# V rows gathered as 32 tokens of four experts, and multiplied in four column groups of 32

## The reference: what is computed

```
for every token t:
    i[0:128], gate[0:128] = top experts of 8 heads x 16, softmax within a head
    w[e] = gate[e] * gelu(dot(u[i[e]], xn[t]))          # 128 weights
    out[t] = sum over e of w[e] * v[i[e]]               # 128 rows of v
```

## Time and profile before

| | |
|---|---|
| median of the timed runs | 2024.65 us |
| fastest, slowest | 2023.76, 2026.74 us |
| span of the profiled execution, first to last instruction | 2043.0 us |
| PE, DVE, ACT, POOL busy | 95%, 58%, 22%, 43% |
| DMA over the span | 300 GB/s |
| share of the chain that ended last: PE, DMA, DVE, POOL | 65%, 13%, 9%, 7% |

### The profile page before, as it was taken

How to read it: one execution, slowest core, us unless ns; L and a number is a source line. 1 busy time by engine, 2 the same in 40 slices (tenths; PEclk the granted TensorE clock), 3 DMA queues, 4 the chain that set the end, 5 groups by cost and what they waited for, 6 DMA issues and landing times.

```text
span 2043.0 us, 23964 instructions
## 1 busy us (share of the span) xinstructions
PE 1942.4 (95%) x9007; PEld 1255.0 (61%) x9007; DVE 1190.6 (58%) x2972; ACT 445.9 (22%) x1045; POOL 870.7 (43%) x785
## 2 busy tenths in 40 slices
PE   8999999999889999999998888999999989999998
PEld 7688886956775887885676765444445543333332
DVE  1022101003896888788899989887867775444321
ACT  2233211111202454121211354000013321101112
POOL 0000000000684423445658355844557776666543
PEclk9999999999999999999999568999999999999999
DMA  7543454434999877999899677999999999999997
GB/s 237 147 121 109 148 155 144 145 103 136 373 388 349 280 255 239 369 386 388 331 359 371 221 261 243 410 409 409 409 376 348 344 334 410 409 409 409 409 389 278
DMA packets 252439, 613.48 MB, mean 300 GB/s; under 512 B 18676, under 2 KB 121124, under 8 KB 252324
## 3 DMA queue, kind: packets, MB, share of 16 engines
q0 software_dynamic: 110592, 402.70, 52.5%
q1 hardware_dynamic: 141120, 208.17, 29.7%
q10 hardware_dynamic: 612, 1.07, 0.2%
HBM read 609.77 MB, written 2.10 MB: 300 GB/s over the span
## 4 chain that ended last, share of the span: by engine, by line
PE 65%; DMA 13%; DVE 9%; POOL 7%; issue 3%; another core or an unknown queue 1%; ACT 1%; SPq 0%; POOLq 0%; DVEq 0%; ACTq 0%
PE ps L617 26%; PE ps L896 11%; PE ps L846 8%; DMA u_rows<-in_peer_u_dram,idx 7%; PE ps L632 7%; POOL u_rows L576 5%; DVE u_rows L1391 4%; PE ps L886 3%; PE ps L659 3%; POOL v_rows L590 2%; DMA wring<-in_w_in_dram 2%; DMA v_rows<-in_peer_v_dram,idx_turned 2%; PE ps L646 1%; PE ps L685 1%
## 5 line engine op out<-in xcount | busy, mean ns | idle before, releaser
L576 POOL DMA_INDIRECT u_rows<-in_peer_u_dram,idx x512 | 584.5, 1142 | 977.1 <-DVE idx L1378 508.2
L1391 DVE CUSTOM_DVE_ANT_0 u_rows<-u_rows,xn 128x1024 f32<-128x1024 f32 x512 | 621.3, 1217 | 177.8 <-DMA u_rows<-in_peer_u_dram,idx 165.2
L617 PE MATMUL ps<-xT,wring 128*128 128x256 f32 x2432 | 553.1, 386 | 22.3 <-DMA wring<-in_w_in_dram 10.1
L617 PEld LDWEIGHTS ps<-xT,wring 128*128 128x128 f32 x2432 | 464.0, 193 | 90.8 <-DMA wring<-in_w_in_dram 11.0
L896 PE MATMUL ps<-d_rows,gates 128*128 128x512 f32 x1024 | 456.3, 600 | 0.8 <-issue 0.8
L896 PEld LDWEIGHTS ps<-d_rows,gates 128*128 128x128 f32 x1024 | 190.7, 191 | 266.6 <-issue 266.6
L846 PE MATMUL ps<-v_rows,diag 64*64 64x512 f32 x1928 | 256.9, 633 | 18.9 <-DMA v_rows<-in_peer_v_dram,idx_turned 16.4
L590 POOL DMA_INDIRECT v_rows<-in_peer_v_dram,idx x121 | 135.4, 1119 | 131.3 <-PE ps L846 98.6
L886 PEld LDWEIGHTS ps<-hot_b,hot_a 128*128 128x128 f32 x1024 | 147.2, 230 | 55.4 <-issue 36.0
L886 PE MATMUL ps<-hot_b,hot_a 128*128 128x64 f32 x1024 | 155.0, 318 | 19.3 <-DVE hot_b L1458 11.0
L1091 ACT ACTIVATE diag<-ident,wgt 128x64 f32<-128x64 f32 x256 | 75.8, 336 | 435.6 <-PE ps L846 351.5
(11 more groups left out here) (201 smaller groups left out, 1747.0 us busy)
## 6 DMA issues: line engine op xcount, KB each, us to landing
wring<-in_w_in_dram SPq DMA_DIRECT2D x128, 512.0 KB
d_rows<-in_peer_v_dram SPq DMA_DIRECT2D x128, 512.0 KB
wring<-in_peer_w_query_dram SPq DMA_DIRECT2D x32, 512.0 KB
wring<-in_w_branch_conv_dram SPq DMA_DIRECT2D x16, 512.0 KB
wring<-in_w_branch_attn_dram SPq DMA_DIRECT2D x16, 512.0 KB
wring<-in_w_out_dram SPq DMA_DIRECT2D x16, 512.0 KB
wring<-in_xattn_wq_dram SPq DMA_DIRECT2D x16, 512.0 KB
wring<-in_xattn_wo_dram SPq DMA_DIRECT2D x16, 512.0 KB
```

The source lines that it names most:

```text
L576: pool.indirect_dma_start(out=u_rows[:, n % URING, :], out_offset=None, in_=peer_u[0], in_offset=bass.IndirectOffsetOnAxis(ap=experts_of(g ...
L617: mm = pe.matmul(bank(job)[:, 0:HN], w[:, k % 4, P * b:P * (b + 1)], act[:, k, :], start=(k == 0), stop=(k == KT - 1))
L1391: dve.tensor_tensor_reduce(out=u, in0=u, in1=(xn2 if h else xn1)[:, i, :], scale=1.0, scalar=0.0, op0=ALU.mult, op1=ALU.add, accum_out=dot ...
```

## The change

Four V rows are now multiplied at a time (`expert_quad`). V row m of a group no longer holds one expert for 128 tokens. Partition 32q + t of row b of set s (m = 4s + b in the group) holds expert 4q + s of token 32b + t: 32 tokens with four experts each. Its weights stand below each other as four 32x32 diagonals, one tile of 128 rows and 32 columns (`ident32`, scaled by ACT). The matmul with the row sums four experts for 32 tokens and writes PSUM partitions 32b to 32b + 31; the four rows of a quad write the four column groups. A token tile now takes two banks, and the two tiles take different banks.

For this the expert numbers (`idx_quad`) are rearranged by 16 small copies of DVE a group instead of two, the weights by 16 small activations of ACT a group (`spread_weights`), and DVE's three multiplies at the end of `gelu` become one. DVE's step 4 of the next group's `gelu` waits for those activations. `diag` has 12 places of half the width. The V ring has 6 places, 8 from slot 108 of this half, 10 from slot 236, and the U places at the end as before. A place comes free when its quad is done. Diagonals are not made before the slot in which their group's weights are spread (`WEIGHTS_AT`). The slots of chunks, blocks and V rows stay; a quad stands in the slot of its fourth row.

```diff
@@ -167,7 +167,8 @@
     HG = GROUPS // 2
-    URING, VRING, DRING, GRING, IRING = 8, 8, 8, 4, 8
+    URING, VRING, DRING, GRING, IRING = 8, 10, 12, 4, 8
+    BLOCK = P // 4
     CHUNKS, BLOCKS = 64, 128
@@ -184,22 +185,25 @@
     FIN_SLOT = {2: HSTEPS + 225}
-    V_OF, DIAG_OF, PAIR_OF = {}, {}, {}
+    V_OF, DIAG_OF, QUAD_OF = {}, {}, {}
+    WEIGHTS_AT = [HSTEPS + TOPK * (g + 1) + 8 for g in range(HG)]
     for m, slot in enumerate(V_SLOT):
         V_OF.setdefault(slot + V_AHEAD, []).append(m)
-        DIAG_OF.setdefault(slot + (DIAG_BEHIND if slot >= STEPS - 16 else -DIAG_AHEAD), []).append(m)
-        if m % 2:
-            PAIR_OF.setdefault(slot, []).append(m - 1)
-
-
-    V_LATE = next(m for m in range(HSTEPS) if V_SLOT[m] >= CH_SLOT[32])
+        DIAG_OF.setdefault(max(slot + (DIAG_BEHIND if slot >= STEPS - 16 else -DIAG_AHEAD), WEIGHTS_AT[m // TOPK]),
+                           []).append(m)
+        if m % 4 == 3:
+            QUAD_OF.setdefault(slot, []).append(m - 3)
+
+
+    V_GROWS = {next(m for m in range(HSTEPS) if V_SLOT[m] + V_AHEAD > TOPK * (HG + PH * (n + 1) - 1)): n
+               for n in range(HT)}
     V_LAST = next(m for m in range(HSTEPS) if V_SLOT[m] + V_AHEAD >= STEPS + 6)
...
     for m in range(HSTEPS):
-        if m == V_LATE:
-            ring = [("v", n, None) for n in (6, 7)] + ring
+        if m in V_GROWS:
+            ring = [("v", 6 + 2 * V_GROWS[m] + n, None) for n in range(2)] + ring
         if m == V_LAST:
@@ -275,8 +279,8 @@
         probsT = at("probsT", [P, 2, XH, HN], 122)
-        diag = at("diag", [P, DRING, P // 2], 122)
-        ident64 = at("ident64", [P, P // 2], 125)
+        diag = at("diag", [P, DRING, BLOCK], 122)
+        ident32 = at("ident32", [P, BLOCK], 123.5)
         hot_b = at("hot_b", [P, 2, 8, 64], 126)
@@ -325,7 +329,7 @@
         idx = tiny("idx", [P, IRING, TOPK], U32)
-        idx_turned = at("idx_turned", [P, HG, TOPK // 2], 125.25, U32)
+        idx_quad = at("idx_quad", [P, HG, TOPK], 125, U32)
         idx2 = at("idx2", [P, HG, TOPK], 124, U32)
@@ -382,7 +386,8 @@
         idx_rdy = sem("idx_rdy")
-        turned = sem("turned")
+        quad_idx = sem("quad_idx")
+        quad_wgt = sem("quad_wgt")
         gate_rdy = sem("gate_rdy")
@@ -486,7 +491,7 @@
         def wait_used(eng, m):
-            eng.wait_ge(v_used, m // 2 + 1)
+            eng.wait_ge(v_used, m // 4 + 1)
@@ -565,8 +570,12 @@
                     wait_job(pool, JOB[("xo", 1, 1)] + 1)
-                    pool.tensor_tensor(ident64[:, :], ident[:, 0:P // 2], ident[:, P // 2:P],
+                    pool.tensor_tensor(ident32[:, :], ident[:, 0:BLOCK], ident[:, BLOCK:2 * BLOCK],
                                        ALU.add).then_inc(iotas, 1)
+                    for q in (2, 3):
+                        pool.wait_ge(iotas, q + 1)
+                        pool.tensor_tensor(ident32[:, :], ident32[:, :], ident[:, BLOCK * q:BLOCK * (q + 1)],
+                                           ALU.add).then_inc(iotas, 1)
                 if n < STEPS:
@@ -585,11 +594,10 @@
                     if e == 0:
-                        pool.wait_ge(turned, 2 * (g + 1))
-                    own = idx_turned[:, g, e // 2:e // 2 + 1] if e % 2 else idx2[:, g, e:e + 1]
+                        pool.wait_ge(quad_idx, 16 * (g + 1))
                     pool.indirect_dma_start(
                         out=v_row(m), out_offset=None, in_=peer_v[0],
-                        in_offset=bass.IndirectOffsetOnAxis(ap=own, axis=0)
+                        in_offset=bass.IndirectOffsetOnAxis(ap=idx_quad[:, g, e:e + 1], axis=0)
                     ).then_inc((v_ready if kind == "v" else u_ready)[place], 16)
@@ -830,22 +838,18 @@
-            def expert_pair(m):
+            def expert_quad(m):
                 if m == 0:
                     pe.wait_ge(wt_done, 2 * SBH)
-                if m == HSTEPS // 2:
-                    pe.wait_ge(hadd, 2)
-                pe.wait_ge(diag_rdy, m + 2)
-                for k in (m, m + 1):
-                    wait_row(pe, k)
-                first, last = m % (HSTEPS // 2) == 0, m % (HSTEPS // 2) == HSTEPS // 2 - 2
+                tile, n = m // (HSTEPS // 2), m % (HSTEPS // 2)
+                pe.wait_ge(diag_rdy, m + 4)
+                for b in range(4):
+                    wait_row(pe, m + b)
                 for c in range(2):
-                    for k, turn in ((m, 0), (m + 1, 64)):
-                        for r in (0, 64):
-                            o = (r + turn) % P
-                            mm = pe.matmul(ps[o:o + 64, 2 * (r // 64) + c, :], diag[r:r + 64, k % DRING, :],
-                                           v_row(k)[r:r + 64, BANK * c:BANK * (c + 1)],
-                                           start=first, stop=last)
+                    for b in range(4):
+                        mm = pe.matmul(ps[BLOCK * b:BLOCK * (b + 1), 2 * tile + c, :], diag[:, (m + b) % DRING, :],
+                                       v_row(m + b)[:, BANK * c:BANK * (c + 1)],
+                                       start=(n == 0), stop=(n == HSTEPS // 2 - 4))
                 mm.then_inc(v_used, 1)
@@ -905,8 +909,8 @@
                     table_transposes()
-                for m in PAIR_OF.get(tau, []):
-                    expert_pair(m)
+                for m in QUAD_OF.get(tau, []):
+                    expert_quad(m)
                 for ch in range(CHUNKS):
@@ -1080,15 +1084,23 @@
+            def spread_weights(g):
+                act.wait_ge(wgt_rdy, HG + g + 1)
+                for b in range(4):
+                    for q in range(4):
+                        to = wgt[BLOCK * q:BLOCK * (q + 1), g, :].rearrange("p (s b) -> p s b", b=4)[:, :, b]
+                        qw = act.activation(to, gl[BLOCK * b:BLOCK * (b + 1), 3, 4 * q:4 * (q + 1)], ACT.Copy)
+                qw.then_inc(quad_wgt, 1)
+
             def diagonal(m):
...
                 if e == 0:
-                    act.wait_ge(wgt_rdy, HG + g + 1)
+                    act.wait_ge(quad_wgt, g + 1)
                 if m == 0:
-                    act.wait_ge(iotas, 3)
+                    act.wait_ge(iotas, 5)
                 if m >= DRING:
-                    act.wait_ge(v_used, (m - DRING) // 2 + 1)
-                act.activation(diag[:, m % DRING, :], ident64[:, :], ACT.Copy,
+                    act.wait_ge(v_used, (m - DRING) // 4 + 1)
+                act.activation(diag[:, m % DRING, :], ident32[:, :], ACT.Copy,
                                scale=wgt[:, g, e:e + 1]).then_inc(diag_rdy, 1)
@@ -1128,7 +1140,7 @@
                 else:
-                    act.wait_ge(hadd, 2 * (i + 1))
+                    act.wait_ge(hadd, i + 1)
                 inverse_rms(("fin", h, i), hbuf[:, t, :], xn2[:, 0, :])
@@ -1146,6 +1158,8 @@
                     take_tables()
+                if tau in WEIGHTS_AT:
+                    spread_weights(WEIGHTS_AT.index(tau))
                 for m in DIAG_OF.get(tau, []):
@@ -1379,9 +1393,12 @@
                     dve.wait_ge(idx_rdy, g + 1)
-                    odd = idx2[:, g - HG, :].rearrange("p (e two) -> p e two", two=2)[:, :, 1]
-                    for r in (0, 64):
-                        dve.tensor_copy(idx_turned[64 - r:P - r, g - HG, :], odd[r:r + 64, :]).then_inc(turned, 1)
+                    for b in range(4):
+                        for q in range(4):
+                            to = idx_quad[BLOCK * q:BLOCK * (q + 1), g - HG, :].rearrange("p (s b) -> p s b", b=4)
+                            dve.tensor_copy(to[:, :, b], idx2[BLOCK * b:BLOCK * (b + 1), g - HG,
+                                                              4 * q:4 * (q + 1)]).then_inc(quad_idx, 1)
+                        yield
@@ -1414,6 +1431,8 @@
                     dve.wait_ge(gate_rdy, g + 1)
+                    if g > HG:
+                        dve.wait_ge(quad_wgt, g - HG)
                     dve.tensor_tensor(s3, a, gate_e[:, r:r + wide, :], ALU.mult)
@@ -1430,13 +1449,8 @@
                     else:
-                        for odd, p0, turn in ((0, slice(0, P), 0), (1, slice(0, 64), 64), (1, slice(64, P), -64)):
-                            to, a3, a2 = (t[:, k, :].rearrange("p (e two) -> p e two", two=2)[:, :, odd]
-                                          for t, k in ((wgt, g - HG), (s3, 0), (s2, 0)))
-                            ins = dve.scalar_tensor_tensor(out=to[p0.start + turn:p0.stop + turn, :], in0=a3[p0, :],
-                                                           scalar=gate_r[p0, 0:1], in1=a2[p0, :],
-                                                           op0=ALU.mult, op1=ALU.mult)
-                        ins.then_inc(wgt_rdy, 1)
+                        dve.scalar_tensor_tensor(out=s3[:, 0, :], in0=s3[:, 0, :], scalar=gate_r[:, 0:1],
+                                                 in1=s2[:, 0, :], op0=ALU.mult, op1=ALU.mult).then_inc(wgt_rdy, 1)
@@ -1460,13 +1474,10 @@
             def add_experts(i):
```

(9 more changed lines are left out.)

## The result

The changed kernel takes 2043.5 us (median of 7 runs, 2037.6 to 2047.0), the kernel before beside it 2027.3 us (7 runs, 2023.8 to 2037.9). The ratio is 1.0077, 95% interval 1.0059 to 1.0095: 0.8% slower. The forecast was 2001 us, 24 us faster, with a range of 1984 to 2023. The time moved the other way, and 2043.5 lies outside the range.

A forecast was written before the change was run, and what follows sets the result against it. It took PE, packed, and DMA, full at 409 GB/s, as two coinciding limits. Terms 0 + 0 + 15 + 11 + 1.2 - 3 gave 24 us: 2024.65 - 24 = 2001 us, range 1984 to 2023.

The forecast's parts named there:

- Quads four abreast: PE's V matmuls: a quad's 8 matmuls take a pair's 1.88 us, 120 us in all instead of 241.
- 409 GB/s as the ceiling: Dense stages: DMA is full at 409 GB/s, so PE's saved time there mostly doesn't shorten them.
- Second dense stage and last rows, -11: From 1678 us: the same 140.4 MB at 409 GB/s take 343 instead of 356 us; 11 of the 13 taken.
- Second chunks, -15: Second gate chunk stage, 1503 to 1678 us: 160 us instead of 175, a gain of 15.
- ring of fours: Rival: V places returned in fours take the second chunk stage's gain; 2016 us, between 2010 and 2033; chance 18%.
- The ring's cycle: Second chunk stage: issue, landing and use take 7.7 us a quad, 162 us in all; 8.6 with chunks ahead, 181.
- Spreading, 3 us in the run-up and 0 beyond: DVE's copies of expert numbers cost 3 us before the first chunks; elsewhere they and ACT's activations cost 0.
- first chunk stage: First gate chunks, 1133 to 1268 us: between a gain of 5 and a loss of 5; 0 taken.
- ACT's part at 0: 16 small ACT activations a group, 54 us in all, stay hidden; 0 taken, 14 us if uncovered in the chunk stages.
- The clock as rival: Rival: less V work lowers PE's granted clock in the second chunk stage, sign under 0.7; 2038 us; chance 5%.
- The tail, -1.2: After PE's last V matmuls DVE adds once instead of twice, 1.24 us each: a gain of 1.2.
- First dense, 0: First dense blocks, 1268 to 1503 us: DMA full, same bytes, so 0.

The follow-up runs named there:

- e10: Changed kernel with V rows 0 to 127 as pairs as before, rows 128 to 255 as quads: 2036.3 us, 0.9974 of the kernel before.
- e5: Kernel before with a U ring of 6 instead of 8 and two V places more (8, later 10): 2042.2 us, 1.0077 of the kernel before.
- e6: Changed kernel with a U ring of 6 instead of 8 and two V places more (8, 10, 12): 2049.2 us, 1.0108 of the kernel before.
- e1: Kernel before, its pairs started by fours at the fourth row's slot and places given back in fours: 2079.9 us, 1.0186 of the kernel before.
- e12: Kernel before plus only the 14 more DVE copies for each of 16 groups: 2051.4 us, 1.0054 of the kernel before.
- e9: Kernel before plus the spreading alone (14 DVE copies, 16 ACT activations a group, into unread places): 2056.7 us, 1.0071 of the kernel before.
- e13: Kernel before plus only the 16 small ACT activations for each of 16 groups: 2040.3 us, 0.9998 of the kernel before.
- e3: Changed kernel with two idle-time matmuls ahead of each quad in both chunk stages: 2062.0 us, 1.0103 of the kernel before.
- e14: Changed kernel without the spreading, indices and weights used as they lie: 2045.4 us, 1.0009 of the kernel before.
- e11: Changed kernel measured again, nothing edited: 2049.7 us, 1.0039 of the kernel before.
- e2: Changed kernel with every quad's 8 matmuls done twice, first into the other tile's banks: 2080.2 us, 1.0187 of the kernel before.

## Why the prediction was wrong

*Quads four abreast: right.* 16 records in 1.92 us where the forecast had 1.88. One at a time they would have taken 7.3 us. The Trainium skill (TensorE: Matmul & The Clock Gate, Part 3: Packing small matmuls, The mechanism) says that a weight load overlaps matmuls in flight only when its row group differs; a quad's four tiles use all rows, and the 1.92 us disagree.

*409 GB/s as the ceiling: right.* PE is busy 309 of the last 356 us where it was packed, and the slices stay at 409. The 435 of the Trainium skill (DMA: Bandwidth & Descriptors, Specifications) is reached in no slice of any run here.

*Second dense stage and last rows, -11: mis-sized.* Measured -2.8 (-1.5, -3.0 and -3.9 by trace). The forecast's full gain was 409 GB/s over the whole stretch. The mean rate rose from 394 to 400 only, as the last 59 us run at 367 (were 331); by an estimate from these rows that is 8 us of the 13. And the step took the bytes as fixed: 297 x 407 + 59 x 367 us give 142.5 MB after 1678 us, where they were 140.4. Part of that is where the stage begins. By the gathers that POOL begins in it, 203 or 204 in the three traces of the changed kernel and 200 to 202 in the four of before, two or three rows of 0.52 MB more are left for it, some 3 us. That this is the ring, which gives back in fours, is not tried by itself; e10 with 140.2 MB from 1671 us (297 x 408 + 54 x 353) took 350.6 us.

*Second chunks, -15: the step that failed.* Measured +4.8 (-0.7, +1.8 and +13.3 by trace): the rival "ring of fours", with PE and POOL waiting for each other in turn. The ring's cycle had been worked out at 7.7 us a quad, or 8.6 with a chunk ahead; measured is 8.35. The forecast then took 160 us, "by POOL's own pace and the ring's", though 155 and 162 to 181 aren't near each other and the slower one decides. Two things can have made the 7.7 too short, and no run parts them: a chunk stands ahead of a quad more often than not (32 chunks among 21 quads), and the sum had the quad at 1.9 us where those that had waited long take 3.64, which alone gives 8.6 as well: (7.6 + 5.9 + 3.6) / 2. e5 and e6 show the ring as the bound, e1 what fours cost with the old matmuls. Nor was PE the chain of this stage before the change: its pairs were 22% of it, the landing of V rows 20%, POOL's gathers 24%. Only in the last 350 us was it PE alone, and there DMA was full beside it.

*Spreading, 3 us in the run-up and 0 beyond: mis-sized and misplaced.* Measured in the run-up +1.9, no more than the starts scatter (1125.8 to 1133.1 for one kernel); in the first chunk stage +4.6, where the forecast had 0 with 9.6 us of DVE idle as cover. That idle time was no cover: most of that stage's chain runs over DVE, and in e12 5.2 us of copies lie on it whole and the stage is some 7 us longer. Alone the spreading costs 0.7% (e9, 0.45 to 0.96); taken out of the changed kernel it gives 0.3% (1.0039 to 1.0009, known to about 0.3). Whether its cost simply adds to the ring's these intervals don't tell. ACT's part at 0 was right (e13).

*The clock as rival: half its condition came.* The granted clock in the second chunks fell from 0.96 to 0.77, not under the 0.7 that was to be its sign. The stage took 174 to 188 us, not the 197 of all work at half clock, and e3 lifted the clock with no gain.

*The tail, -1.2: right,* one addition instead of two. *First dense, 0: right* (+0.6).

*The sum.* By stages it was to be -24 us and came to +8: 20 of the 32 us between them are the second chunks, 8 the last stages, 5 the first chunks. On chips where the kernel before takes 2040 to 2042 us that is the whole difference: fours +1.9% (e1), shorter work of a quad -1.8% (e1 to e14), spreading +0.3% (e14 to e11), together the 0.4 that e11 measured. These are steps from one kernel to the next (before, e1, e14, e11), so that they add up proves nothing; what stands by itself is e2, by which the shorter work is worth 1.5%. On a chip where the kernel before takes 2027 the changed kernel is 0.8 to 1.1% slower, and 2043.5 lies outside the ring rival's 2010 to 2033 too. No trace of the kernel before comes from such a chip, so where the other 0.4 to 0.7% stand is open. So is why the second chunk stage of one kernel takes 174 us in one execution and 188 in another.

## What to carry to other kernels

Where an engine's work is cut by taking more rows at once, work out the ring's cycle (issue, landing, use, return of the whole set) with the new grain before counting the engine's saving, and take the slowest of the paces, not a value between them. Idle time of an engine in a stage is no cover for new work if that engine is most of the stage's chain: 9.6 us of idle in 135 hid little or nothing of 5 us of copies. And a change can be worth making in the stages that it helps alone: half of this one is 0.3% faster where the whole, beside the same runs, is 0.4% slower.

## What the runs showed of the hardware

Four 128x32 stacks of weights in four column groups, all on the same 128 rows, run four abreast: 16 records of 512 columns in 1.92 us at the full clock, 3.64 at half. Small DVE copies (32x4) take 0.163 us (median), and eight in a row 1.65 to 1.75 us; fourteen more of them a group, 16 groups in all, cost 0.54% of the time (e12). The same unchanged kernel has medians from 2026.6 to 2041.7 us on different chips, 0.7%, as much as the effect in question (one chip, measured twice, gave 2040.3 and 2041.6). Runs side by side are needed, and even their ratio moved with the chip: 1.0110 and 1.0039 for the same two kernels.
